# Block two's mixer: other steps for the convolution's taps, shorter retention chains, and a spread end of the convolution

## The reference

```
p = h @ w_in                      # rq rk rv rg | gq gf gi gg | ca cb | gates
# retention, 4 heads of 128: rotary q and k, decayed causal scores, times v
q, k = rope(rq), rope(rk);  o = retention(q, k, rv)
o = (o - mean(o)) * rsqrt(mean((o - mean(o))**2) + eps);   u_a = o * g * silu(rg)
# hgrn, 4 heads of 128: gated linear recurrence with forget gate f(gf)
o = hgrn2(silu(gq), log f, 1 - f, gi)
o = o * rsqrt(mean(o**2) + eps);                           u_b = o * g * silu(gg)
# causal depthwise convolution over 31 taps on 512 channels, layer norm, silu
u = dwconv(ca * sigmoid(cb), conv_w) + conv_b;             u_c = silu(layer_norm(u))
y = sigmoid(g0)*(u_a @ wb0) + sigmoid(g1)*(u_b @ wb1) + sigmoid(g2)*(u_c @ wb2)
out = y @ w_out
```

## Time and profile before

| what | value |
|---|---|
| median of the three runs shown | 3538.58 us (3537.52 to 3539.75) |
| the profiled execution, its own time | 3535.84 us |
| its span | 3534.0 us |
| TensorE matmuls busy | 3346.2 us, 95% |
| VectorE busy | 2132.8 us, 60% |
| ScalarE busy | 1305.6 us, 37% |
| GpSimd busy | 610.7 us, 17% |
| mean granted TensorE clock | 0.984 |

### The profile page before, as it was taken

How to read it: one execution, slowest core, us unless ns; L and a number is a source line. 1 busy time by engine, 2 the same in 40 slices (tenths; PEclk the granted TensorE clock), 3 DMA queues, 4 the chain that set the end, 5 groups by cost and what they waited for, 6 DMA issues and landing times. The chain is left out here.

```text
span 3534.0 us, 38828 instructions
## 1 busy us (share of the span) xinstructions
PE 3346.2 (95%) x15296; PEld 2666.8 (75%) x15296; DVE 2132.8 (60%) x2709; ACT 1305.6 (37%) x1684; POOL 610.7 (17%) x488
## 2 busy tenths in 40 slices
PE   8899999999999999989999898999899999989997
PEld 6577788886678788867777786888677777768885
DVE  8853666448644765476556746555675558465545
ACT  4664322235663322223322325333433322343333
POOL 2222222121212312201001132010210001320002
PEclk9999999999999999999999999999999999999999
DMA  3022555321224454232112222222221112222221
GB/s 135 33 68 84 185 192 197 112 96 53 58 66 155 176 196 157 84 105 72 60 54 72 78 102 91 96 96 90 78 72 65 57 58 90 89 72 97 99 101 61
DMA packets 72180, 344.43 MB, mean 97 GB/s; under 512 B 25152, under 2 KB 26048, under 8 KB 35648
## 3 DMA queue, kind: packets, MB, share of 16 engines
q1 hardware_dynamic: 70416, 339.12, 27.5%
q0 software_dynamic: 576, 2.33, 0.2%
q10 hardware_dynamic: 1008, 0.51, 0.0%
HBM read 340.51 MB, written 2.10 MB: 97 GB/s over the span
## 5 line engine op out<-in xcount | busy, mean ns | idle before, releaser
L881 PE MATMUL bank<-Hhi_b,whi_b 128*128 128x512 f32 x2976 | 1218.4, 409 | 60.6 <-ACT Hhi_b L2009 22.1
L882 PE MATMUL bank<-Hhi_b,wlo_b 128*128 128x512 f32 x2976 | 1169.4, 393 | 0.0
L888 PE MATMUL bank<-Hlo_b,whi_b 128*128 128x512 f32 x2976 | 1159.5, 393 | 0.8 <-DVE Hlo_b L2289 0.8
L859 DVE TENSOR_TENSOR wlo_b<-raw_b,whi_b 128x2048 fp32r<-128x2048 f32 (+2 forms) x290 | 625.9, 2158 | 480.8 <-ACT whi_b L853 480.4
L881 PEld LDWEIGHTS bank<-Hhi_b,whi_b 128*128 128x128 f32 x2976 | 565.6, 190 | 210.6 <-issue 41.2
L882 PEld LDWEIGHTS bank<-Hhi_b,wlo_b 128*128 128x128 f32 x2976 | 565.7, 190 | 124.9 <-issue 13.7
L888 PEld LDWEIGHTS bank<-Hlo_b,whi_b 128*128 128x128 f32 x2976 | 563.2, 189 | 125.0 <-DVE Hlo_b L2289 4.5
L853 ACT ACTIVATE whi_b<-raw_b 128x2048 fp32r<-128x2048 f32 (+2 forms) x290 | 511.6, 1764 | 368.9 <-PE bank L888 365.0
L881 PE MATMUL bank<-Uhi_b,whi_b 128*128 128x512 f32 x1024 | 408.4, 399 | 23.7 <-ACT sg_b L934 15.9
L882 PE MATMUL bank<-Uhi_b,wlo_b 128*128 128x512 f32 x1024 | 402.0, 393 | 0.0
L888 PE MATMUL bank<-Ulo_b,whi_b 128*128 128x512 f32 x1024 | 388.0, 392 | 0.0
(11 more groups left out here) (250 smaller groups left out, 3463.2 us busy)
## 6 DMA issues: line engine op xcount, KB each, us to landing
raw_b<-in_w SPq DMA_DIRECT2D x234, 1024.0 KB, 4.9
ada_b<-in_wada SPq DMA_DIRECT2D x48, 1024.0 KB, 6.9
raw_b<-in_w SPq DMA_DIRECT2D x40, 512.0 KB, 3.6
raw_b<-in_w SPq DMA_DIRECT2D x16, 768.0 KB, 4.3
rel_b<-in_rel SPq DMA_DIRECT2D x128, 24.0 KB, 2.4
X_keep<-in_x SPq DMA_DIRECT2D x4, 512.0 KB, 9.3
decay_b<-in_decay POOLq DMA_DIRECT2D x2, 1024.0 KB, 6.5
out<-X_keep SPq DMA_DIRECT2D x8, 256.0 KB, 2.0
```

The costliest lines, as they stand in the source:

```text
L859: self.nc.vector.tensor_tensor(self.wlo[n % RAW_SLOTS][:, 0:words], self.raw[n % RAW_SLOTS][:, 0:words], self.whi[n % HI_SLOTS][:, 0:words ...
L881: self.nc.tensor.matmul(out, whi[:, k, cols], xhi, start=(k == 0), stop=False)
L882: self.nc.tensor.matmul(out, wlo[:, k, cols], xhi, start=False, stop=False)
L888: mm = self.nc.tensor.matmul(out, whi[:, k, cols], xlo, start=False, stop=(k == nk - 1))
```

## The change

- `taps_beside` returns 1 beside a step that holds one hgrn level alone, where it returned 0.
- In layer 0, `gap` gets `free` 0 behind the pieces of panels 1 and 2 (panel 0 has no gap).
- A retention head has nine steps in place of eleven: `vt2` joins `rrot rk`, and `rscore` 2 and 3 are one step.
- In the list `conv`, markers "rest" stand between `cmean` and `css` and between `css` and the `cfin`, two each: a marker takes the rest of its gap and does nothing.
- What is left in `conv` at the start of branch 2 is run by `gap(2)`.

```
     if group[0][2] == "r":
         return 1 if "oss" in kinds else 2
-    return 0
+    return int(kinds == ["level"])
...
             for _ in range(taps_beside(step(), free)):
                 if conv:
-                    run(conv.pop(0))
+                    item = conv.pop(0)
+                    if item[0] == "rest":
+                        break
+                    run(item)
...
                 if i == 3:
-                    conv.extend([("cmean", l), ("css", l)] + [("cfin", l, c) for c in range(4)])
+                    conv.extend([("cmean", l), ("rest",), ("rest",), ("css", l), ("rest",), ("rest",)])
+                    conv.extend(("cfin", l, c) for c in range(4))
...
-                    first = [(item("rrot", "rq"),), (item("rrot", "rk"),), (item("vt2"),)]
-                    first += [(item("rscore", j),) for j in range(TT)] + [(item("rpv"),), (item("omean"),)]
+                    first = [(item("rrot", "rq"),), (item("rrot", "rk"), item("vt2")), (item("rscore", 0),)]
+                    first += [(item("rscore", 1),), (item("rscore", 2), item("rscore", 3)), (item("rpv"),), (item("omean"),)]
...
                 while conv:
-                    run(conv.pop(0))
+                    gap(2)
...
-                        gap(3 if kind == "z" else 2)
+                        gap(0 if l == 0 and i < 3 else 3 if kind == "z" else 2)
```

## The result

The changed kernel takes 3550.21 us (median of five runs, 3546.26 to 3555.43) against 3538.58 (five runs, 3535.03 to 3541.59): ratio 1.0031, 95% interval 1.0021 to 1.0042, slower by 11.6 us. The range of the prediction holds it; its likeliest case, +1.9 us with 3533 to 3549 and no difference to be told, does not. The profiled execution took 3554.90 us with a span of 3553.1.

What follows compares the result with a forecast made beforehand. It took TensorE, busy 95% of the span, as the bound, so only waits and half clock could change. Terms of -6.4 us in layer 0 and +8.3 in layer 1 gave +1.9; forecast 3540.5 us, range 3526 to 3552.

Steps and rivals of the forecast that it cites:

- likeliest case: Whole kernel: total +1.9 us, forecast 3540.5, bounds 3533 to 3549; chance 0.56.
- First panels: Layer 0, panels 1 and 2 without taps: panel 3's wait falls to 0.8, head 0's score wait shrinks; -13.4 us.
- Retention head 1: Both layers: its score, wanted one slot sooner, waits 5.1 us plus 1.6 of half clock; +6.7 each.
- Head 3: Retention head 3 waits 5.1 us in layer 0 and 4.3 in layer 1; -0.7 and -1.4.
- Head 2: Retention head 2 waits 0.5 us in place of 1.9 (layer 0) and 3.1 (layer 1); -1.4 and -4.2.
- Head 0 of layer 1: Retention head 0 keeps its 21 early taps; its score, wanted 3.2 us sooner, waits 3.2; +4.8 with the clock.
- hgrn: Hgrn heads wait 2.8 us at level 2: head 0 newly, +4.4 a layer; head 1 loses other waits, -1.7 a layer.
- Taps beside levels: 25 taps a layer beside hgrn levels fit in DVE's free time; 0 us, bounds -0.5 and +2 a layer.
- css -1.5, cfin +1.2 a layer: Convolution's end: css loses its 1.5 us wait; the cfin wait moves from panel 37 to panel 34, becoming 8.8.
- The clock: TensorE behind most waits over 2 us: a half-clock stretch of 3.41 us costs 1.6 us.
- Rival 1: New waits bring half-clock stretches of 6.8 us, not 3.4, each costing 1.6 more; 3553 us, chance 0.20.
- The signs: Panel 3 waits under 1 us, retention scores 5 or 3, four level waits of 2.8, css none, panel 34 9.

## Why the prediction held where it did, and where it failed

- **First panels, -13.4:** right; -15.0 alone. Waits, half clock and head 0's score went as worked out.
- **Retention head 1, +6.7 a layer:** right. Waits of 4.26 and 4.47 for 5.1, busy half clock of 4.80 and 5.55 us for 3.41 (2.2 and 2.6 for 1.6): +6.5 and +7.1. Part of the agreement is luck: the span of 16.2 us, copied from head 2 of before, held a 0.59 us wait for GpSimd and a key operation of 1.73 us where it takes 0.69 elsewhere. Head 1 of after has neither, but a split of 3.37 us for 2.29.
- **Head 3, 5.1 and 4.3:** right, 4.94 and 4.47; its half clock cost 2.4 to 2.5 where I put 1.6.
- **Head 2, 0.5 with no half clock: the term that failed.** Measured 6.32 + 2.8 and 7.87 + 2.3, so 18.3 us more than the sum had; its bounds for this wait were 0 and 2. The sentence at fault is "Head 2 has three slots of taps ahead and no end step in its way". I took DVE to be free at slot 20 and counted from there. But I had counted slots, not DVE's queue: head 1's end step does lie there, the split of a panel waits for it, and the taps of three slots, nine by `free` = 3, stand behind the split. One tap a slot takes the wait down to 0.23 and 1.18.
- **Head 0 of layer 1, +4.8:** 2.74 with 3.41 us of half clock, +4.3: right.
- **hgrn, +4.4 and -1.7 a layer:** right for head 0 (2.79 and 2.78); head 1 went to 2.79 as said, and a small wait of 0.49 on head 0's values came in that the sum did not have.
- **Taps beside levels, 0:** right, +0.1 alone.
- **css -1.5, cfin +1.2 a layer:** the wait moved to panel 34 as said and is 8.0 for 8.8 (in layer 1 it stood at 8.38 in before, where the sum took layer 0's 7.57 for both). But the two terms are one: alone the part moves nothing (+0.4), since the 1.5 taken from css come back in the wait behind it.
- **The clock.** Rival 1 (long stretches) did happen behind heads 1 to 3 of both layers, but its price of 1.6 more each was too high: it was 0.6 to 1.2 more. Its time of 3553 is near the result by luck: the larger part of the result is head 2, of which it had only 2 us of wait. The argument against it was weak: the 3.86 us wait that ends at 1912.15 in before already had a stretch of 6.83 us (1911.52 to 1918.35), with TensorE busy in 6.20 of them.
- **The signs** that the prediction listed came true (panel 3 waits 0.24, four waits of 2.8 to 2.9 a layer at the levels, none of css, 8.0 at panel 34). None of them was about head 2; the backlog of taps was looked for at the levels only.

The terms of the heads came to -6.1 and +8.6 us by the prediction; measured are +0.6 and +17.3 between the two traces, 15.4 more, and head 2's two terms alone were 18.3 too low. That the medians differ by only 9.7 from the forecast is owed to the rest of the mixer, 3.8 better for 0.6 predicted, and to a profiled execution above its median. So it is partly luck that the range, with its end at 3552, holds the result.

**GpSimd beside DVE.** In after, around head 2's pile, three GpSimd and three DVE instructions overlap (the timeline joins some of them; these are the single ones). They end one behind the other: GpSimd's residual of the end step at 1631.24, a tap at 1631.78, the first multiply at 1632.93, the split at 1635.08, the second multiply at 1636.24, the next tap at 1636.79. The taps took 1.66 and 1.78 us where the others took 0.75, the split 3.37 for 2.28. In before the split of head 2 began 0.06 us ahead of the multiply and took 2.29; the multiply took 3.39 for 1.26. The Trainium skill (SBUF — State Buffer, "Who interferes with whom") says that a Vector instruction with two SBUF inputs contends with a GpSimd instruction that reads SBUF, and that the lock is exclusive. By that rule the trace agrees. Which of the two is first can't be read off the records to a few hundredths: a tap whose record begins 0.02 us ahead of GpSimd's (1645.77) took 1.82 us, and GpSimd's multiply its 1.26. The rule was weighed for the levels and dropped; there too it agrees, for no tap beside a level overlaps a GpSimd instruction in the run with these taps alone.

So the DVE work ahead of head 2's gate was some 3 us longer than its instructions alone. Taking the taps away ended the wait with the GpSimd multiplies still in place (the split took 2.93 there), so they add to the pile and do not alone cause the wait; they were not tried apart.

## What to carry to other kernels

Spare work in "empty" slots of a hand-made order is only free if the engine's queue has drained by then: count the work that stands in the queue at the slot, not the slots. When a small product waits, ask what stands ahead of the rounding that its input waits behind: work that nobody is waiting for (an end step, a final scaling) belongs behind it. A shorter chain should be judged again once the order around it is mended: the same nine-step head cost 30 us in one order and was worth 18 in the other.

## What the runs showed of the hardware

- A stretch at the 1.2 GHz level began up to 6.0 us before the wait ahead of it had ended (1998.67 against 2004.63; 1647.10 against 1651.32 at head 2). In the mixers of after, stretches of 3.41 us stand at waits of 2.7 to 3.5, 6.83 at 4.3 to 4.9, and 10.24 at 6.3 to 8.0 (once 6.83 at 8.03). In the run with one tap in empty slots this is otherwise: 3.41 at a wait of 4.94, 6.83 at one of 2.78. The sums above agree if only the part in which TensorE is busy is priced.
- Not every wait has one: hgrn head 2's 2.78 us in layer 0 of after was followed by full clock, head 1's 2.79 by 3.41 us at half.
- The same code gets a different share of half clock from one execution to the next: before 1500 us, in block one, TensorE was busy at half clock for 6.8 us in the trace of before and 19.6 in that of after.
- A GpSimd multiply that took 1.26 us at 1645.78 (where the tap beside it took 1.82) took 1.74 and 3.34 us beside DVE's work at head 2 of after: the second began at 1632.90, inside a DVE split, and ended 1.16 us after it.
